# Feed-forward part of a decoder layer: the last pass by token chunks, with the second layer norm inside it

## The reference, cut to what matters

```
def layer_norm(x, g, b):
    mu = mean(x); var = mean((x - mu) ** 2)          # over the 1024 columns of a token
    return (x - mu) * rsqrt(var + 1e-5) * g + b

u = x * (1 + sc_f) + sh_f
f = (silu(u @ w_gate) * (u @ w_up)) @ w_down
x = layer_norm(ALPHA * x + (1 + g_f) * f, ln2_g, ln2_b)      # ALPHA = 2 ** 0.25
```

## Time and profile before

| what | value |
|---|---|
| median of 3 runs | 1912.36 us (1908.15 to 1912.43) |
| the profiled execution's own time | 1921.81 us |
| its span, first to last instruction | 1920.0 us |
| mean granted TensorE clock | 0.92 of full |
| TensorE busy | 1630.2 us (85% of the span) |
| VectorE, ScalarE, GpSimd busy | 921.0, 555.4, 271.5 us |

### The profile page before, as it was taken

One profiled execution on the slowest core, in us unless ns is written; L12 is line 12 of the kernel. 1 busy time (PEld: TensorE's weight loads), 2 busy tenths in 40 slices (PEclk: granted clock), 3 DMA queues, 4 the chain that ended last, 5 costly groups with the idle time before them and its releaser, 6 DMA issues. The chain is left out here.

```text
span 1920.0 us, 32274 instructions
## 1 busy us (share of the span) xinstructions
PE 1630.2 (85%) x13265; PEld 1450.1 (76%) x13265; DVE 921.0 (48%) x1705; ACT 555.4 (29%) x1084; POOL 271.5 (14%) x262
## 2 busy tenths in 40 slices
PE   5698898459799688878698389999999999999981
PEld 2354444249799677767598389999999999999981
DVE  2577677263333466676437724334433333442337
ACT  0143344332111255565424321121121111112123
POOL 3023434500000112222113200000000000000006
PEclk8799899769899789999799689999999999999995
DMA  9489896230121000000222041121112112112013
GB/s 369 192 325 367 337 367 254 75 102 20 51 55 33 20 14 11 5 14 1 80 99 86 27 129 34 34 66 33 43 56 66 33 33 66 33 33 66 1 66 133
DMA packets 116504, 183.59 MB, mean 96 GB/s; under 512 B 17039, under 2 KB 86359, under 8 KB 112301
## 3 DMA queue, kind: packets, MB, share of 16 engines
q1 hardware_dynamic: 106428, 101.71, 16.8%
q0 software_dynamic: 8192, 75.85, 9.9%
q10 hardware_dynamic: 1776, 4.51, 0.7%
HBM read 172.06 MB, written 9.94 MB: 95 GB/s over the span
## 5 line engine op out<-in xcount | busy, mean ns | idle before, releaser
L1979 PE MATMUL ps<-mix_conv,wf_hl 128*128 128x384 f32 (+1 forms) x1584 | 272.5, 321 | 11.7 <-DVE wf_hl L2004 11.7
L1979 PE MATMUL ps<-mix_attn,wf_hl 128*128 128x384 f32 (+1 forms) x1584 | 270.9, 319 | 0.0
L1979 PEld LDWEIGHTS ps<-mix_conv,wf_hl 128*128 128x128 f32 x1584 | 255.2, 189 | 11.8 <-DVE wf_hl L2004 11.8
L1979 PEld LDWEIGHTS ps<-mix_attn,wf_hl 128*128 128x128 f32 x1584 | 253.7, 188 | 0.0
L1993 PE MATMUL ps<-hid,wd_hl 128*128 128x384 f32 (+1 forms) x1584 | 249.9, 318 | 0.0
L1993 PEld LDWEIGHTS ps<-hid,wd_hl 128*128 128x128 f32 x1584 | 248.8, 188 | 0.0
L2019 DVE TENSOR_TENSOR h<-ps,gate 128x384 f32<-128x384 f32 (+1 forms) x66 | 34.1, 516 | 320.3 <-PE ps L1979 320.3
L2034 DVE TENSOR_TENSOR acc<-ps,acc 128x384 f32<-128x384 f32 (+1 forms) x240 | 123.7, 516 | 93.4 <-PE ps L1993 93.2
L1648 POOL TENSOR_TENSOR ln_y<-ln_y,ln_g 128x1024 f32<-128x1024 f32 (+3 forms) x18 | 38.1, 2117 | 902.9 <-ACT ln_y L1638 902.8
L625 DVE STREAM_TRANSPOSE rows_T<-ring 128x1024 f32<-128x1024 f32 x128 | 150.3, 1213 | 29.1 <-DMA ring<-in_cache_latent,idx 25.5
L1055 PE MATMUL ps<-U,wc_hl 128*128 128x384 f32 (+1 forms) x864 | 138.3, 323 | 8.6 <-DVE wc_hl L1069 8.6
(11 more groups left out here) (321 smaller groups left out, 2440.6 us busy)
## 6 DMA issues: line engine op xcount, KB each, us to landing
ring<-in_w_ada SPq DMA_DIRECT2D x12, 2048.0 KB, 10.3
wf_raw<-in_w_gate SPq DMA_DIRECT2D x22, 512.0 KB, 4.0
wf_raw<-in_w_up SPq DMA_DIRECT2D x22, 512.0 KB, 5.3
wd_raw<-in_w_down SPq DMA_DIRECT2D x22, 512.0 KB, 5.9
wc_raw<-in_w_in SPq DMA_DIRECT2D x24, 256.0 KB, 3.1
x_nat<-in_x_prompt SPq DMA_DIRECT2D x4, 1024.0 KB, 7.8
wo_raw<-in_w_o SPq DMA_DIRECT2D x8, 512.0 KB, 4.3
ln_x<-in_x_prompt SPq DMA_DIRECT2D x8, 512.0 KB, 4.2
```

The source lines that it names most:

```text
L1979: last = pe.matmul(ps[:, 2 * (q % 2) + g, 0:tn], a, x, start=j == 0, stop=j == 3 * KD - 1)
```

## The change

The last pass is taken out of `turns` and written by chunks. For each chunk: gate/up of block 0, gate/up of block 1, then its eight down products. The down products keep their four banks 4 to 7. The layer norm of chunk c is put into the work of chunk c + 1, in the same block, without a barrier: its turns stand between and behind the gate/up steps and use the bank pairs 4 and 6, and the down products wait until the sums of these tiles have left them (`norm.summed`). `stats` is split into `sum` and `moments`; the moments and factors of two of three tiles stand between VectorE's additions. Chunk 2's tiles follow at the end. GpSimd does all 1024 columns of tiles 0 to 5, and 768 of tiles 6 to 8. The weight splits of the last down block move behind the first hidden path. Tile buffers are three deep instead of four and lie where the raw weights lay, so SyncE loads them once the last splits are done.

The diff, cut to its core (in `affine` only counts and columns change; `sum` and `moments` are the two halves of `stats`):

```diff
@@ Norm @@
+    def sum(self, dve, t, freed):
...
+    def moments(self, dve, t):
...
+    def affine(self, eng, t, on_pool, cols=None, first=0):
...
@@ phase_ffn, sync @@
+                    body(LAST, False, True)
+                    sp.wait_ge(gu_lo, NF * 2)
+                    sp.wait_ge(d_lo, NF)
+                    norm.load_x(sp, 0)
+                    norm.load_gb(sp)
+                    norm.load_x(sp, 1)
+                    norm.load_x(sp, 2)
+                    for t in range(9):
...
+                        sp.wait_ge(norm.done, t + 1)
+                        wait(sp, norm.done_dve, t - 5)
+                        sp.dma_start(dst, norm.y[0:rows, t % 3]).then_inc(stored[t % 3], 16)
+                        if t + 3 < 9:
+                            norm.load_x(sp, t + 3)
@@ gpsimd @@
+                    for t in range(9):
+                        norm.affine(pool, t, True, cols=D if t < 6 else 768)
@@ scalar @@
+                    split_gu_hi(act, NF - 1, LAST, 1, False)
+                    for c in range(3):
+                        if c:
+                            gate_z(c - 1)
+                        hidden(c, 0)
+                        if c == 0:
+                            for s in range(2):
+                                act.wait_ge(d_in[s], LAST * 16 + 16)
+                                act.wait_ge(down, LAST * 24)
+                                act.activation(wd[:, s, 0], raw_d[:, s], ACT.Copy).then_inc(d_hi, 1)
+                        else:
+                            norm.root(act, 3 * c - 3)
+                        hidden(c, 1)
+                        if c:
+                            norm.scale(act, 3 * c - 3)
+                            normal(3 * c - 2)
+                            normal(3 * c - 1)
+                    gate_z(2)
+                    for t in CHT[2]:
+                        normal(t)
@@ tensor @@
+                    for c in range(3):
+                        if c == 0:
+                            pe.wait_ge(gu_lo, NF * 2 - 2)
+                        gate_up(c, 0)
+                        if c == 0:
+                            pe.wait_ge(gu_lo, NF * 2)
+                        else:
+                            turn_z(3 * c - 3)
+                            turn_z(3 * c - 2)
+                        gate_up(c, 1)
+                        if c:
+                            turn_z(3 * c - 1)
+                            pe.wait_ge(norm.summed, 3 * c)
+                        if c == 0:
+                            pe.wait_ge(d_lo, NF)
+                        pe.wait_ge(h_lo, LAST * 6 + 2 * c + 2)
+                        for m in range(KD):
+                            down_sum(c, m)
+                    for t in CHT[2]:
+                        turn_z(t)
@@ vector @@
+                    for c in range(3):
+                        t = 3 * c - 3
+                        hidden(c, 0)
...
+                        else:
+                            norm.sum(dve, t, freed)
+                            norm.sum(dve, t + 1, freed)
+                            norm.moments(dve, t)
+                        hidden(c, 1)
+                        if c:
+                            norm.factors(dve, t)
+                            norm.sum(dve, t + 2, freed)
+                        for m in range(KD):
+                            add(c, m)
+                            if c and m in (1, 4):
+                                norm.moments(dve, t + (1 if m == 1 else 2))
+                            if c and m in (2, 5):
+                                norm.factors(dve, t + (1 if m == 2 else 2))
+                    dve.wait_ge(added, LAST * 24 + 24)
+                    dve.tensor_tensor(acc[:, :, SEQ:], acc[:, :, SEQ:], modT[:, 5 * KD:, 0:NS], ALU.mult).then_inc(zs_gated, 1)
+                    for t in CHT[2]:
+                        norm.sum(dve, t, freed)
+                        norm.moments(dve, t)
+                        norm.factors(dve, t)
+                        if t > 6:
+                            norm.affine(dve, t - 1, False, first=6)
+                    norm.affine(dve, 8, False, first=6)
```

177 lines of the change are left out of this document (108 added, 69 removed).

## The result

The change made the kernel faster: 1897.74 us, median of six runs (1892.31 to 1903.54), beside 1910.03 for the kernel before, median of six too (1908.15 to 1912.43). The ratio is 0.9934, 95% interval 0.9915 to 0.9954, so 12.3 us less. The forecast was 1899.4 with a range of 1894 to 1906.

The account below looks back on a forecast made before the run. TensorE is full in the last pass, but nothing is full in the 59.54 us layer-norm tail behind it. Saving 15.0 less 2.0 for the clock gives 13: 1912.4 − 13 = 1899.4 us, range 1894 to 1906.

Parts of the forecast that it names:

- In its words: Last matmul to tile-6 sum falls from 37.1 to about 8 us, while the last pass grows by about 14.
- First two stands: TensorE waits before the down products of chunks 0 and 1, for hidden remainder, factors and sum: 2.0 and 2.8 us.
- The wait of 0.7: In chunk 2, turns of tiles 3 and 4 wait 0.7 us for ScalarE's eight gate scalings, ending at 1856.3.
- Third stand: TensorE waits 4.0 us before chunk 2's down products: table load, late second SiLU, remainder, factors, sum of tile 5.
- The clock: Granted clock falling behind TensorE's stands: 0.8 us for the first two, 1.2 for the third, 2.0 off the saving.
- From the last addition on: Tile 5's scaling, eight gate scalings (3.28 us) and a half-clock turn (1.8) lead from about 1877.7 to 1883.2.
- Tail from the tile-6 sum: Old tail's 22.6 us less one VectorE affine pair of 0.85 ahead of tile 7: 21.8 us.
- A: Rival: clock falls at every stand, or once for long; price 4 to 8.5 us, saving 5 to 10; chance 0.13.
- C: Rival: TensorE never regains its clock after the first stand; price up to 45 us, end 30 later; chance 0.03.
- B: Rival: GpSimd holds VectorE's hidden remainders in chunk 2, up to 2.4 us twice; saving 8; chance 0.06.
- D: Rival: a table switch costs twice its 1.28 us load for the two on the path, 2.6 later; chance 0.04.
- E: Rival: no clock fall in chunks 0 and 1, VectorE's waits overlap better; saving 15 to 17 us; chance 0.12.

Follow-up runs that it names:

- the fillers: Changed kernel with TensorE transposing the identity into a free bank while it would stand; from last pass's first matmul to span's end 110.58 us.
- the fastest version: Changed kernel plus moved roots and gate scalings, chunk 2 statistics together, identity transposes, earlier loads, GpSimd whole on tile 6; median 1886.78 us, ratio 0.9865 to the kernel before.

## Why the prediction was right

The forecast was 13 us less; 13.8 were found in S and 12.3 in the timed runs. The medians came out 1.7 below the forecast because the kernel before measured 1910.03 this time and not 1912.36 (2.3), less 0.7 of saving. Its walk through the pass, step by step, in us from the pass's first matmul:

| step | predicted | measured |
|---|---|---|
| products of chunk 0 start | 18.8 | 18.89 |
| products of chunk 1 start | 49.2 | 50.92 (49.4 with no fall before them) |
| turns of tiles 3, 4 wait for | 0.7 | none |
| products of chunk 2 start | 76.3 | 76.89 |
| last addition ends | 85.5 | 86.23 |
| tile-6 sum starts | 91.0 | 92.08 |
| end | 112.8, with the clock 114.8 | 114.06 |

- **In its words**: TensorE's last matmul 14 later, and from it to the tile-6 sum about 8 (its own times give 8.9). Measured: 16.4 later, which is the 14 and the clock, and 7.6. Its 37.1 for the old way is counted from the end of the matmul row (1860.26), not from the 1860.46 that it names.
- **First two stands**: 2.0 and 2.8 predicted, 1.84 and 2.37 in the rows; the second is ended by the sum of tile 2, as foreseen.
- **The wait of 0.7** for the gate scalings is not there. They ended at 1845.60, and the turns started at 1845.85, right behind the step. The additions of chunk 1 ended 0.9 earlier than I had them, once the fall of the clock is allowed for.
- **Third stand**: 4.0 was too much, 3.03 in the row. The mechanism is the one named, remainder, factors, sum, behind a table load ahead of SiLU. Moving the root and the factors shortened it to 1.70, leaving out the loads to 2.02.
- **The clock**: 2.0 taken, 3.5 measured by the fillers. For the first two stands I took 0.8, and it was 1.6 in each of the nine traces with turns and no fillers. Which of the two stands it follows changes from execution to execution, so 0.8 for half a fall each had no better ground than 1.6. Of the 3.5, 0.9 is the half-clock turn of the tail, which the sum had already. The rest, 2.6 (1.6 and 1.0 behind the third stand, where I took 1.2), is to be set beside my 2.0. So the walk without the clock was 1.2 to 1.3 too long (112.8 against 114.06 less 2.6), by the third stand and the wait of 0.7 above all, and the clock was 0.6 too small.
- **From the last addition on**: tile 5's scaling, 3.28 of gate scalings, turn at half clock: predicted 5.5, measured 5.85.
- **Tail from the tile-6 sum**: 21.8 predicted, 21.98 measured, but by errors that cancel, which is luck. The rows of before that it rests on, VectorE behind the tile-6 sum and the sum of tile 8:

```profile
1900.95 1.05 DVE L1648 TENSOR_TENSOR ln_y<-ln_y,ln_g 128x256 f32<-128x256 f32 x1
...
1908.91 1.21 DVE L1610 SCALAR_TENSOR_TENSOR ln_y<-ln_x,ps 8x1024 f32<-8x1024 f32 x1 [1.96 <-PE ps L1598]
```

From tile 6's sum to tile 7's it was 4.98 in before, and 3.57 in after. I had taken 0.85 off for the pair of halves that goes; that pair began with one of 1.05, so 1.41 went. From tile 7's sum to tile 8's it was 6.54 and became 7.27. There the wait of 1.96 for the turn is gone, since the turns come early, but VectorE's halves of tile 6 meet GpSimd's and take 1.85 and 1.91. I had expected GpSimd to have ended its sixth tile before tile 6 came, and it had (1874.1); that it and VectorE would meet on tile 6 itself I had not.

**The rivals.** A (clock falls at every stand, or once for long, 4 to 8.5) does not hold: there is one fall in the first two and one behind the third, and 3.5 in all. Its saving of 5 to 10 also does not follow from its price, which in place of the 2 would leave 6.5 to 11. C (the clock never comes back) is excluded by the window of chunk 1 at 1.00. B (remainders held by GpSimd) did not occur in the four remainders of after, 0.56 and 0.43 each, though the third started only 0.3 us behind GpSimd's last instruction (1848.32 and 1847.98); that it can is seen in the kernel without the square root (1.30). D (a switch costs more than its load) is excluded: where the instruction behind a load had its input, it follows 0.02 us later (1824.04 + 1.28, then 1825.34), and leaving out all loads brought 1.4. The Trainium skill, "ScalarE: Activation LUTs", "What ACT_TABLE_LOAD costs", has about 2.66 us for every switch, of which 1.38 is the drain (its advice to do one set's calls together stands in the page's next section, "Table sets: the hidden batching unit"). No switch of this kernel shows the drain, and the measurement decides. E (15 to 17 saved) needed stands without a fall of the clock. With the turns in the pass only the fillers gave that, and with them S is 17.3 under before.

**What I had not seen**: what the alternatives would be. The chunk order lengthens the pass by 5.9 us and is paid back by early gate scalings, whose worth I had not set apart. And ScalarE's queue held up the end: its gate scalings behind tile 5, with the statistics spread, cost about 5 us as the change has them; once the root and the gate scalings are moved, the spreading itself costs only 0.4. Both stood in the walk as terms. The growth of the pass itself was less of a choice: in the fastest version the last addition still ends at 83.95 where after has 86.23. That version's other gains are the way from there to the tile-6 sum, 1.73 instead of 5.85, and the tail behind it, 19.96 instead of 21.98.

## What to carry to other kernels

When work of a later stage is put beside the matmuls of an earlier one, walk the queue of every engine that serves both: here the end of the program waited for ScalarE's queue order and then for SyncE's and GpSimd, not for the engine that the spreading was to protect. Compare profiled executions over the stretch that was edited; here it repeated to 0.1 us while the start of that stretch moved by up to 20. And a removed wait is worth only the distance to the next one: behind ScalarE's came a load held by GpSimd's backlog, for which VectorE stood 1.05 to 1.35 us.

## What the runs showed of the hardware

- **Short stands and the clock.** In every kernel without fillers that had turns in the pass, the granted clock fell from its upper level (1.00, 2.4 GHz) to the lower (1.2 GHz) behind one of the first two stands, of 1.84 to 2.4 us, and cost 1.56 us each time; which of the two it was changed between two executions of the same kernel. Behind the third stand it fell when that was 2.02 to 3.18 us and not when it was 1.70 or 1.71. The kernel with the chunk order alone, with stands of 1.84, 1.80 and 1.45, had no fall. The same length can go either way: 1.84 was followed by a fall in three of ten cases, and a wait of 2.13 in the middle of chunk 2's products by none, while two of 1.93 there were.
- **Fillers.** Transposes that nobody reads kept the clock at 1.00 behind each stand that they filled (S 3.5 less in after); they did nothing for a wait of 1.93 us elsewhere (granted clock 0.62 behind it).
- **VectorE beside GpSimd.** An instruction of VectorE that reads both inputs from SBUF and meets a running one of GpSimd ended 0.3 us behind it: 0.42 became 1.85 and 1.91 in after, 0.43 became 1.30 in the kernel without the root. Additions that read PSUM kept their 0.56 and 0.43 beside GpSimd throughout. The Trainium skill, "SBUF — State Buffer", "Who interferes with whom", says that a VectorE instruction with two SBUF inputs contends with a GpSimd instruction that reads SBUF, that one with at most one SBUF input does not (outside certain modes), and that the port pair they share is an exclusive lock. The trace agrees, with these numbers.
- **Table loads** ran 1.28 us each in front of their instruction, often while that instruction was still waiting for its input (1819.32 in after, 4.5 us ahead of its root at 1823.82); such a load adds nothing.
